# Attention scores and value products in two passes instead of three, with high and low parts stacked in the 128 rows

## The reference

```
z = q @ k.T / 8                                   # stick-breaking heads
log_1m = where(s < t, log_sigmoid(-z), 0);  tail = reverse_cumsum(log_1m) - log_1m
a = where(s < t, exp(log_sigmoid(z) + tail), 0);  out_sb = a @ v
logits = q @ k.T / 8 + F[t] - F[s], F = cumsum(log f);  s <= t      # forgetting heads
out_fx = softmax(logits) @ v
merged = [rms_norm(out_sb), rms_norm(out_fx)] @ w_out
```

## Time and profile before

| | |
|---|---|
| median of 3 runs | 1140.4 us (1140.26 to 1140.91) |
| the profiled execution, its own time | 1141.62 us |
| its span, first to last instruction | 1139.9 us, mean granted clock 0.987 |
| TensorE busy | 1095.4 us, 96% |
| VectorE busy | 631.0 us, 55% |
| ScalarE busy | 512.0 us, 45% |
| mixer tiles | 424.6 to 657.3 us of the span |
| in them: TensorE, VectorE, ScalarE busy | 227.5, 174.8, 162.4 us |

### The profile page before, as it was taken

How to read it: one execution, slowest core, us unless ns; L and a number is a source line. 1 busy time by engine, 2 the same in 40 slices (tenths; PEclk the granted TensorE clock), 3 DMA queues, 4 the chain that set the end, 5 groups by cost and what they waited for, 6 DMA issues and landing times.

```text
span 1139.9 us, 15601 instructions
## 1 busy us (share of the span) xinstructions
PE 1095.4 (96%) x5066; PEld 910.7 (80%) x5066; DVE 631.0 (55%) x1049; ACT 512.0 (45%) x917; POOL 21.1 (2%) x36
## 2 busy tenths in 40 slices
PE   7999999999999799999999896999999999999897
PEld 5888888888888578888888784788888888888785
DVE  6454445444224877777778768744544545333744
ACT  5433333333223555766667734533333334333536
POOL 5000000000010000000000000000000000000000
PEclk9999999999999899999999997999999999999999
DMA  5333333332333222222211121333333244444002
GB/s 183 94 95 95 98 95 93 98 102 94 100 93 92 65 65 61 51 55 55 52 38 35 38 70 50 98 93 102 92 98 96 83 129 129 154 131 138 1 19 74
DMA packets 99011, 97.02 MB, mean 85 GB/s; under 512 B 7136, under 2 KB 82976, under 8 KB 98976
## 3 DMA queue, kind: packets, MB, share of 16 engines
q1 hardware_dynamic: 98976, 96.56, 28.7%
HBM read 94.44 MB, written 2.10 MB: 85 GB/s over the span
## 4 chain that ended last, share of the span: by engine, by line
PE 87%; DVE 7%; ACT 4%; issue 1%; DMA 0%; DVEq 0%; SPq 0%; ACTq 0%
PE bank L1127 28%; PE bank L1128 27%; PE bank L1129 27%; PE bank L1363 2%; DVE acc L773 1%; DVE scratch L1068 1%; DVE scratch L792 1%; DVE xT L797 1%; DVE w_r L753 1%; PE bank L1147 1%; PE bank L1394 1%; DVE scratch L1090 0%; PE bank L1156 0%; DMA scratch<-in_x 0%; ACT rms L453 0%
## 5 line engine op out<-in xcount | busy, mean ns | idle before, releaser
L753 DVE TENSOR_TENSOR w_r<-w_raw,w_r 128x512 fp32r<-128x512 f32 x332 | 227.0, 692 | 385.1 <-ACT w_r L432 384.9
L432 ACT ACTIVATE w_r<-w_raw 128x512 fp32r<-128x512 f32 x332 | 205.5, 629 | 426.4 <-PE bank L1129 426.1
L1127 PE MATMUL bank<-xg,w_r 128*128 128x512 f32 x890 | 350.0, 393 | 1.5 <-DVE xg L779 1.5
L1129 PE MATMUL bank<-xg,w_r 128*128 128x512 f32 x890 | 346.6, 389 | 0.0
L1128 PE MATMUL bank<-xg,w_r 128*128 128x512 f32 x890 | 346.4, 389 | 0.0
L1127 PEld LDWEIGHTS bank<-xg,w_r 128*128 128x128 f32 x890 | 167.3, 188 | 38.6 <-DVE xg L779 4.3
L1129 PEld LDWEIGHTS bank<-xg,w_r 128*128 128x128 f32 x890 | 167.1, 188 | 35.5
L1128 PEld LDWEIGHTS bank<-xg,w_r 128*128 128x128 f32 x890 | 167.4, 188 | 34.2 <-issue 0.5
L1127 PE MATMUL bank<-big,w_r 128*128 (+1 forms) x416 | 162.8, 391 | 0.3 <-DVE xg L957 0.3
L1129 PE MATMUL bank<-big,w_r 128*128 (+1 forms) x416 | 161.9, 389 | 0.0
L1128 PE MATMUL bank<-big,w_r 128*128 (+1 forms) x416 | 161.9, 389 | 0.0
(11 more groups left out here) (168 smaller groups left out, 1042.8 us busy)
## 6 DMA issues: line engine op xcount, KB each, us to landing
w_raw<-in_ffn_w_gate SPq DMA_DIRECT2D x88, 256.0 KB, 2.8
w_raw<-in_ffn_w_up SPq DMA_DIRECT2D x88, 256.0 KB, 2.8
w_raw<-in_ffn_w_down SPq DMA_DIRECT2D x88, 256.0 KB, 2.7
w_raw<-in_w_in SPq DMA_DIRECT2D x36, 256.0 KB, 2.8
scratch<-in_w_ple_gate SPq DMA_DIRECT2D x16, 256.0 KB, 3.3
w_raw<-in_w_in SPq DMA_DIRECT2D x24, 128.0 KB, 2.3
scratch<-in_x SPq DMA_DIRECT2D x2, 1024.0 KB, 6.6
w_raw<-in_w_out SPq DMA_DIRECT2D x8, 256.0 KB, 3.0
```

The costliest lines, as they stand in the source:

```text
L432: act.activation(w_slot(0, slot, 0, 4 * P), w_raw[:, slot, :], ACT.Copy).then_inc(w_hi, 1)
L753: dve.tensor_tensor(w_slot(1, slot, 0, 4 * P), w_raw[:, slot, :], plain(w_slot(0, slot, 0, 4 * P)), SUB).then_inc(w_lo, 1)
L1127: pe.matmul(dst, w_hi_ap, m_hi, start=start, stop=False, skip_group_check=True)
L1129: return pe.matmul(dst, w_hi_ap, m_lo, start=False, stop=stop, skip_group_check=True)
```

## The change

Per head, one matmul now has hi in 64 of its 128 rows and lo in the other 64.

- Scores: `q_both[hh]` holds q hi in the head's rows and q lo in the other rows; `k_twice[hh]` holds k hi in both; `k_low[hh]` holds k lo in the head's rows and zeros elsewhere. Two passes give hi*hi + hi*lo and lo*hi. For the forgetting heads the empty half of the second pass carries the gate rows (`q_aug`, `k_aug`), so the separate `aug` pass and `aug_rows` go.
- The copies to the other half are DMAs on the SP queue: `double_k` (two per tile) and `double_fx` (eight per tile), placed between the weight loads.
- `qk_split` becomes eight 64-row operations on each of ScalarE and VectorE instead of two 128-row and four 64-row ones.
- Values: v hi and v lo of one head lie side by side in the 128 columns of the stationary operand, so a weigh takes two passes (a hi, a lo). The result has two halves in O_BANK that must be added: ScalarE copies one (`o_half`), VectorE adds the other (`o_added`), both 64 rows, per head and kind. Only in `hh` 1 do ScalarE and VectorE then make `oT` hi, squares, `oT` lo and the sum of squares, on 128 rows.
- On VectorE `out_sum(0)` stays where `out_lo(0)` was; `out_lo(0)` moves behind `pt_lo`. The next `weigh` waits for `o_added`, the last output stage for `o_out`.
- GpSimd sets constants in ten small blocks instead of two large ones, and the `pick` constants go.

```diff
+            def double_k(tile):
+                for hh in range(2):
+                    sp.wait_ge(qk_hi, 8 * tile + 2 * hh + 2)
+                    sp.dma_start(plain(k_twice[hh][others[hh], :]), plain(k_twice[hh][halves[hh], :])).then_inc(k_doubled, 16)
+            def double_fx(tile):
+                if tile == 0:
+                    sp.wait_ge(pad_zero, 10)
+                    sp.wait_ge(f_act, 6)
+                for hh in range(2):
+                    hd = 2 * tile + hh
+                    sp.wait_ge(qk_hi, 8 * tile + 2 * hh + 6)
+                    first = HD * (1 - hh)
+                    sp.dma_start(plain(kf_twice[hh][others[hh], :]), plain(kf_twice[hh][halves[hh], :])).then_inc(fx_doubled, 16)
+                    sp.dma_start(plain(q_aug[hh][halves[hh], :]), plain(qf_both[hh][halves[hh], :])).then_inc(fx_doubled, 16)
+                    sp.dma_start(plain(q_aug[hh][first:first + 2, :]), plain(f4[hd:hd + 33:32, :])).then_inc(fx_doubled, 16)
+                    sp.dma_start(plain(k_aug[hh][first + 32:first + 34, :]),
+                                 plain(f4[64 + hd:64 + hd + 33:32, :])).then_inc(fx_doubled, 16)
+            for tile in range(1, TILES):
                 for j in range(TILE_UNITS):
                     c, kh = divmod(j, 2)
+                    if j == (5 if tile == 1 else 6):
+                        double_k(tile - 1)
+                    if j == 6:
+                        double_fx(tile - 1)
...
@@ scalar: qk_split, out_hi
-                act.activation(full[0], hold[:, c, :], ACT.Copy).then_inc(qk_hi, 1)
                 for hh in range(2):
-                    act.activation(pads[hh][0][halves[hh], :], hold[halves[hh], cp, :], ACT.Copy).then_inc(qk_hi, 1)
+                    act.activation(q[hh][halves[hh], :], hold[halves[hh], cq, :], ACT.Copy).then_inc(qk_hi, 1)
+                    act.activation(k[hh][halves[hh], :], hold[halves[hh], cq + 1, :], ACT.Copy).then_inc(qk_hi, 1)
...
                         act.wait_ge(o_done, 2 * hd + kind + 2)
-                        g = gains[rows, ds(GAIN_AT[gain] + j, 1)]
-                        act.activation(oT[0][rows, ds(j + 4 * kind, 1), :], O_BANK[rows, :].unsqueeze(1), ACT.Copy,
+                        act.activation(o_sum[halves[hh], kind, :], O_BANK[halves[0], :], ACT.Copy).then_inc(o_half, 1)
+                        if hh == 0:
+                            return
+                        act.wait_ge(o_added, 2 * hd + kind + 2)
+                        g = gains[:, ds(GAIN_AT[gain] + j, 1)]
+                        act.activation(oT[0][:, ds(j + 4 * kind, 1), :], o_sum[:, kind, :].unsqueeze(1), ACT.Copy,
                                        scale=g).then_inc(o_hi, 1)
-                        squares(8 * N_SB + 2 * hd + kind, O_BANK[rows, :], rows, kind)
+                        act.wait_ge(added, SQ_AT[N_SB] + 2 * j + kind)
+                        act.activation(o_sq, o_sum[:, kind, :], ACT.Square).then_inc(squared, 1)
...
@@ vector: mixer_tile
-                    if more or hh == 0:
-                        aug_rows(hd + 1)
...
+                    def out_sum(kind):
+                        dve.wait_ge(o_half, 2 * hd + kind + 1)
+                        dve.tensor_tensor(o_sum[halves[hh], kind, :], O_BANK[halves[1], :], o_sum[halves[hh], kind, :],
+                                          ADD).then_inc(o_added, 1)
...
-                    out_lo(0, "sb_group_g")
+                    out_sum(0)
                     for b in range(3):
                         c = slice(512 * b, 512 * b + Z_W[b])
                         dve.wait_ge(pt_hi, 3 * hd + b + 1)
...
+                    out_lo(0, "sb_group_g")
                     unit(4)
                     if hh == 1 and more:
                         v_split(j + 1, 0)
                     project_out(2)
                     unit(5)
+                    out_sum(1)
                     out_lo(1, "fox_group_g")
@@ tensor: mixer_tile
-                            product(dst, kt[0][:, c * P:(c + 1) * P], kt[1][:, c * P:(c + 1) * P],
-                                    q_sb[0][:, c * P:SEQ], q_sb[1][:, c * P:SEQ], at == 0, False)
+                            for k in (k_twice, k_low):
+                                pe.matmul(dst, k[hh][:, c * P:(c + 1) * P], q_both[hh][:, c * P:SEQ],
+                                          start=at == 0 and k is k_twice, stop=False, skip_group_check=True)
...
+                    pe.wait_ge(fx_doubled, 128 * j + 128)
...
-                        product(dst, qf[0][:, b * P:(b + 1) * P], qf[1][:, b * P:(b + 1) * P],
-                                k_fx[0][:, 0:w], k_fx[1][:, 0:w], at == 0, False)
-                        pe.matmul(dst, aug[0][:, b * P:(b + 1) * P], aug[1][:, 0:w], start=False, stop=False, skip_group_check=True)
+                        pe.matmul(dst, qf_both[hh][:, b * P:(b + 1) * P], kf_twice[hh][:, 0:w], start=at == 0, stop=False,
+                                  skip_group_check=True)
+                        pe.matmul(dst, q_aug[hh][:, b * P:(b + 1) * P], k_aug[hh][:, 0:w], start=False, stop=False,
+                                  skip_group_check=True)
...
-                            last = product(O_BANK[:, c * P:SEQ], v[0][:, c * P:(c + 1) * P], v[1][:, c * P:(c + 1) * P],
-                                           a[0][:, first:first + w], a[1][:, first:first + w], c == 0, c == TB - 1)
+                            v = v_cols[kind][:, (2 * c + hh) * P:(2 * c + hh + 1) * P]
+                            for part in range(2):
+                                last = pe.matmul(O_BANK[:, c * P:SEQ], v, a[part][:, first:first + w], start=c == 0 and part == 0,
+                                                 stop=c == TB - 1 and part == 1, skip_group_check=True)
```

More of the change, by code:

```diff
@@ L146, in build @@
         halves = [slice(HD * hh, HD * hh + HD) for hh in range(2)]
[L147 to L152, removed]
+        others = halves[::-1]
+        k_low, q_aug, k_aug, k_twice, q_both, qf_both = ([big[:, 2 * i + hh, :] for hh in range(2)] for i in range(6))
+        kf_twice = [big[:, 16 + hh, :] for hh in range(2)]
+        v_cols = [big[:, 12 + 2 * i:14 + 2 * i, :].rearrange("p r n -> p (r n)") for i in range(2)]
+        v_r = [v.rearrange("p (s h l d) -> p s h l d", s=TB, h=2, l=2) for v in v_cols]
+        o_sum = sq
+        o_sq = rms[:, 1, :]
         wf_r = [big[:, 30:32, :], big[:, 32:34, :]]
@@ L407, in _, with v_source @@
             pool.wait_ge(w_used, U_DOWN[0] + 24)
+            done = 0
             for hh in range(2):
-                pool.memset(plain(big[halves[1 - hh], 4 * hh:4 * hh + 4, :]), 0.0).then_inc(pad_zero, 1)
-            pool.wait_ge(pad_zero, 2)
+                first = HD * (1 - hh)
+                low, high = (slice(first + 32 * i, first + 32 * i + 32) for i in range(2))
+                for block, value in ((k_low[hh][others[hh], :], 0.0), (q_aug[hh][low, :], 0.0), (k_aug[hh][low, :], 1.0),
+                                     (q_aug[hh][high, :], 1.0), (k_aug[hh][high, :], 0.0)):
+                    if done:
+                        pool.wait_ge(pad_zero, done)
+                    pool.memset(plain(block), value).then_inc(pad_zero, 1)
+                    done += 1
+            pool.wait_ge(pad_zero, 10)
             for p in range(2):
                 pool.memset(plain(wf_r[p]), 0.0).then_inc(wf_zero, 1)
-        CONSTS = 13
+        CONSTS = 9
         def w_slot(p, slot, first, size=P):
             return w_r[:, p, slot, first:first + size]
+        def v_source(kind):
+            return (T_BANK, O_BANK)[kind][:, :].rearrange("p (s h d) -> p s h d", s=TB, h=2)
         @block.scalar
@@ L590, in mixer_tile @@
                     hd = 2 * j + hh
-                    rows = slice(HD * hh, HD * hh + HD)
                     def unit(x):
@@ L765, in zero_acc, with add @@
                 dve.memset(acc[:, slot, :], 0.0).then_inc(acc_zero, 1)
-            def add(n_zero, at, slot=0, rows=slice(0, P), par=0):
+            def add(n_zero, at, slot=0, src=None, par=0):
                 dve.wait_ge(acc_zero, n_zero)
@@ L772, in add @@
                     dve.wait_ge(added, at)
-                dve.tensor_tensor(acc[rows, slot, :], acc[rows, slot, :], sq[rows, par, :], ADD).then_inc(added, 1)
+                dve.tensor_tensor(acc[:, slot, :], acc[:, slot, :], sq[:, par, :] if src is None else src, ADD).then_inc(added, 1)
             def low(stage, k, gain):
@@ L1370, in mixer_tile, with weigh @@
                     parts(1)
-                    def weigh(v, a):
+                    def weigh(kind, a):
                         for c in range(TB):
@@ L1414, in _ @@
             down(0)
[L1415 removed]
+            pe.wait_ge(pad_zero, 10)
             mixer_start()
```

114 lines of the change are left out of this document (52 added, 62 removed).

## The result

The changed kernel takes 1144.8 us (median of 5 runs, 1144.4 to 1149.0), the kernel before 1140.8 beside it; the ratio is 1.0046, 95% interval 1.0035 to 1.0058. The forecast was 1139.9, no change. So it is slower, by about 4 to 5 us, though TensorE does less: it is busy for 1081.6 us where it was 1095.4.

What follows compares the result with a forecast made beforehand. Matmul time on TensorE was taken as the bound until a wait replaces it. +1.5 start, -9.9 between boundaries, +4.8 and +4.4 boundaries, -1.3 last tile make -0.5: 1139.9 us, own range 1137.5 to 1142.5, wider range 1133 to 1146.

Steps and rivals of the forecast that it cites:

- The saving: Every head of the mixer: five passes of 0.62 us fewer, 3.1 us a head, 24.8 over eight if all shows.
- The boundary: Odd head's weigh to next tri: waits for VectorE and ScalarE chains lengthen it, +4.8 us for two boundaries, +4.4 at the third.
- The start of tile 0: Before the first logits: late split and eight copies on SP open a gap of 2 us; +1.5 us taken.
- My middle value: Start of tile 0: +1.5 us, taken as the middle between bounds -0.4 and +2.9.
- a low end: Start of tile 0: copy issues at half the load's price, landing within the load's 2.3 us, give -0.4 us.
- the floor of 800 ns: Start of tile 0: a skill's floor for tiny transfers; as landing time it makes the term about 0, the sum -2.0.
- The last tile: From sp_lo on: -2.3 to the next tri, +0.8 to the last weigh, -0.1 and +0.3 behind it; sum -1.3 us.
- The whole saving: Rival, all heads: the 24.8 us saving arrives whole, giving 1115.6 us; chance 9%.
- the cheaper chains: Rival, boundaries and start: split, sums and adds cost less (-3.0 us), start at its low end (-1.9), giving 1135.0; chance 19%.
- The slower one: Rival, boundaries: slow clock falls on tri and project(1) uncovered, 1.6 us at each of three, +4.9, giving 1144.8; chance 23%.
- nothing is hidden for the copies in later tiles: Rival, each tile: the copies don't land under cover, 1 us for each of three tiles, giving 1143; chance 5%.
- PSUM evacuation as the new limit: Mixer heads: a skill's warning, doubted as throughput since VectorE's 21 to 23 us still fit in 26.7 us a head.

Runs made afterwards that it cites:

- e2: Changed kernel with VectorE's and ScalarE's order rewritten at the three tile boundaries, part of the work carried into the next head; 1130.0 us, ratio 0.9908 to before.
- e6: Changed kernel with one edit: TensorE's logits wait for their own head's four copies, not all eight; 1141.7 us, ratio 1.0011 to before.
- e7: Changed kernel with VectorE's second split behind pt_lo and ScalarE's hi and squares of kind 0 behind pt_hi, nothing carried; 1147.8 us, ratio 1.0053 to before.
- e8: Changed kernel with squares, their additions, hi and lo of kind 1 carried into the next head, both splits still first; 1141.1 us, ratio 1.0002 to before.
- e9: Kernel before, unaltered, profiled once more; 1141.2 us.
- e10: Changed kernel, unaltered, third profile; 1147.6 us.
- e1: Changed kernel with two of head 0's copies issued before SP's wait for f_act, logits waiting for their own four copies; 1141.8 us, ratio 1.0007 to before.
- e0: Changed kernel, unaltered, timed and profiled again; 1145.9 us, ratio 1.0042 to before.
- e4: Kernel before plus only the values' part of the change (two-pass weigh, half sums), scores and copies as before; 1141.6 us, ratio 1.0009 to before.

## Why the prediction was wrong

- **The saving** of five passes a head: right. 3.4 to 3.5 us a tile between the boundaries (3.3 forecast), 3.1 a head where nothing waits (e2).
- **The boundary**: right in its mechanism. Weigh to tri 24.6, 24.5, 24.5 against 23.95; half-row operations at 0.72 against 0.70; wait for `pt_lo` 3.17 in two pieces against 3.0. Where it was short: the handoffs between engines, 0.26 us from the end of the sum (483.55 + 0.69) to ScalarE's hi at 484.50, which I had put at 0.05. The low clock behind the first gap falls under the wait for `sp_lo`: e6 and the changed kernel take the same 13.78 us with and without it. e2 shows that it was the order alone, and e7 and e8 that two chains bind one behind the other. The Trainium skill, VectorE: DVE Perf Modes, section "Two Vector instructions with no wait between them", says that an instruction is held until the earlier ones have finished where its operands start in another group of 32 partitions than theirs; the halves alternate here, and the trace agrees: each subtraction lasts 0.69 and the next starts after 0.72, while full rows of 0.68 start 0.60 apart.
- **The start of tile 0: this is the step that failed.** Forecast +1.5, bounds -0.4 to +2.9; measured +3.7, between e9 and e10 +5.2. The time of the first issue was right (426.3), the rest not. An issue of these copies costs 0.57 us, not the 0.373 of a load: 1.6 us over eight, of which a landing 1.7 us after the issue instead of 2.3 gives 0.6 back, so the logits start at 431.99 and not near 431. And the gap of 2.7 us doesn't only cost itself. It keeps the clock at 0.50 through the logits: from them to tri it took 9.47 us where 8.82 less 1.1 was counted, and by e1 this part is 2.1 us. I had left it to the top of the range. My middle value averaged in a low end that no row spoke for (issues at half the price of the one I had), and which by those rows would come to about 0, not -0.4. With the start eased and nothing else, e1 and e6 bring the kernel back to the time of before. The Trainium skill, DMA: Bandwidth & Descriptors, gives in its section "Anatomy of one DMA" a fixed cost of about 2.0 us for a DMA that GpSimd issues. SP issued these, and no run here has one from GpSimd; the 1.7 us from issue to landing of a 4 KB copy are near that figure, and twice the floor of 800 ns that I weighed, which the page gives for a round trip to HBM. By the floor I would have been further off.
- **The last tile**: -3.1 against -1.3, and the two are less alike than that. From its first tri to the weigh it took 8.42 us where it took 7.79, and I had counted no change: the clock fell behind the 2.06 us gap, onto tri (0.64 over 619.62 to 624.30). From there to the next tri it took 14.1 against the 15.4 counted; the weigh that I had put at the slow clock ran at full clock, which is 0.7 of it, and the rest is open. The slow clock that I charged after the 2.7 us gap stayed away in this execution (and came in e10, whose last tile took 40.9).
- **The tail**: +1.9 in untouched code, in two of three profiles (+0.5 in the third). It was not in the forecast, and no operation of the change stands there.
- **The rivals.** The whole saving and the cheaper chains fell with the boundary's 24.6 us. The slower one named the clock at the boundaries and gave 1144.8. That this is the measured number is luck. At the first two boundaries tri doesn't pay for the clock. At the third it does, in all three profiles of the changed kernel: both gaps lower the clock, and from tri to the weigh it takes 8.4 us where e2, with tri at full clock, takes 7.2. That is 1.2 of the rival's 4.9 us. That nothing is hidden for the copies in later tiles is refuted: no boundary shows a wait for them. PSUM evacuation as the new limit is refuted by e2, where VectorE and ScalarE keep up with a TensorE that is busy for the whole of both heads shown.

By the profiles: -0.5, +2.2 (start), +1.1 (boundaries), -0.4 (between), -1.8 (last tile), +1.9 (tail) is the +2.5 of the table. The medians differ by 4.0 and 4.8, more than this pair; e0's profile is 4.3 above before's: 1.2 of it lies before the first norm of the mixer, where the executions scatter (376.6 and 378.1 for the kernel before, 376.3 to 377.9 for the changed one).

What stays open: what decides whether the clock falls behind a given gap, and so how much of the +4 to +5 is owed to gaps of the changed kernel that only now and then cost something. The mean clock of all its timed runs is 0.975 to 0.978, that of before 0.986 to 0.991, which fits that; runs without a profile don't say where.

## What to carry to other kernels

Here fewer matmul passes paid only once the chains that TensorE waits for were reordered too. So write out the order of the other engines at the tightest place, and expect two chains one behind the other, so that mending one may show next to nothing. Work whose result is needed a head later (squares, sums, parts of an output) goes behind the operations that the next matmul waits for. Eight DMA copies inside SBUF cost mostly their issues here, so wait only for the copies that the next matmul reads. And count a gap on TensorE at its length plus the matmuls that may then run at half clock, unless a later wait covers them.

## What the runs showed of the hardware

- The same gap has either outcome. Behind the 2.00 us of the tail the clock fell in 4 of 13 profiles (first profile of after, e0, e7, e8), behind the 2.5 to 2.6 us before the last tri in 4 of 9, and behind the 1.48 us at the start of tile 0 in the first profile of before and in e4, and not in e9. The fall behind 1.76 us from which I took the price of an episode didn't come again in e9 either: the same gap, 1.75 us there, at clock 1.00.
- Issues on SP's queue of copies inside SBUF take 0.46 to 0.60 us each, 4 KB or 128 KB alike, against 0.37 for a weight load.
- A half-row operation on VectorE lasts as long as one on all 128 rows (0.69 and 0.68 us), and the eight of a split, whose halves alternate, start 0.72 apart where full rows start 0.60 apart.
- A low clock costs nothing where a later wait covers it: 13.78 us at clock 0.78 in the changed kernel and at 1.00 in e6.
